# A two-block transformer layer in one kernel: 896 instead of 768 gathered value features, a ring of four blocks, and another order of work where the second block begins

## The chip, the cores and the metric

The kernel runs on one core of a Trainium2 chip. Its time is the device time of one execution in microseconds (us), given as the median of several runs. TensorE (PE in the profile) multiplies matrices and loads their stationary operand (PEld); VectorE (DVE), ScalarE (ACT) and GpSimd (POOL) work on elements; SyncE (SP) issues most DMAs.

## The reference

Two blocks in a row act on 256 tokens of 2048 features. The part that the change touches is the end of the first block, PEER, and the start of the second, in short:

```python
# per token chunk: 8 heads, the 16 best of 16384 experts each
act = jax.nn.gelu(jnp.einsum('chkd,cd->chk', u, zc))     # u = rows of peer_u
v = jnp.take(peer_v, expert, axis=0)
w = (gate * act.astype(jnp.float32)).astype(zc.dtype)
y = jnp.einsum('chk,chkd->cd', w, v)                     # sum of 128 rows of peer_v
...
x = rmsnorm(h + y, norm_f_g)                             # end of the first block
h = rmsnorm_2(x, g_pre_mix)                              # start of the second
proj = jnp.einsum('bsd,de->bse', h, w_in) + b_in
```

## The kernel before

The work is a list of 544 units, walked by every engine in its own program. A unit is one output tile of a matrix product: 1 MB of weights in two halves. SyncE fetches a half into one of eight slots (`raw`); ScalarE rounds it to a high part (`hi`, L997), VectorE subtracts that for a low part (`lo`, L1396), and TensorE multiplies high and low parts with high and low parts of the activations (`ZA`, `ZB`), one pass each. Activations lie feature by feature, 16 tiles of 128 features by 256 tokens (`X` is the residual). An engine's program at step u prepares the weights of units u+2 and u+3 (`prep` in `walk`), evacuates unit u-1, and then does what tables hang on step u.

PEER is computed densely. In the score stage (units 56 to 183) every expert's score is made. In the value stage (units 184 to 311, eight chunks of 16 units) `expert_unit` multiplies scores by `peer_v`, token by token: each unit adds four pieces x to `VM[q]`, for 512 features q, with two halves of 128 tokens (h = 0, 1), and three matmuls each (L670 to L673). The units of a chunk go round q = 0, 1, 2, 3; the last chunk does all of q = 0 first, then 1, 2 and 3, so that q is finished early.

The second token half leaves out its last `WIDE` features: for these GpSimd fetches, for each of 128 picks per token, that token's row of `peer_v` from a copy with rows of `WIDE` features (`v_wide`, made by ScalarE's DMAs in `widen` at the steps of `COPY_AT`) into a ring of `RING` blocks of two rows (`vrow`, `pick`), and VectorE adds them up, weighted, into `vacc` (`picked_dot`, L1727) at the steps of `DOTS_AT`, some units behind the fetches (`picks_by`). `FROM_Q` is the first tile of 128 features that is gathered; for q = 2 the second half has 128 * (FROM_Q - 8) columns left in the matmuls.

At the border, `expert_out(q)` copies the finished sums of q out of PSUM (ScalarE the first token half, L1147, VectorE the second with the gathered sums, L1779 and L1783). `expert_turn(q)` on TensorE (L730, eight transposes) turns them to feature order, after units 300, 304 and 309 and, for q = 3, inside the first group of the second block; `expert_add` adds them to `X` (L1789). `expert_sum(i)` on ScalarE then makes, for each of 16 feature blocks, a square of `X` for the first norm (L1153), `X` times `gf` (L1154), the high operand of the second block from it (L1158), and a square for the second norm (L1161); VectorE makes the low operand (`expert_low`, L1793), GpSimd adds the squares up (`expert_squares`, L2141). The second block starts at unit 312 (`F0`): units 312 and 313 go as a group, k by k, with `expert_turn(3)` after four k. After unit 314 TensorE sums the added squares over the partitions (L755). Semaphores order all of it; an engine that waits holds back everything behind it in its program.

## Time and profile before

| | |
|---|---|
| median of 3 runs | 2969.21 us (2968.11 to 2969.28) |
| profiled execution | 2968.23 us, span 2966.4 us |
| PE / PEld | 2944.9 / 2534.2 us busy |
| DVE / ACT / POOL | 2160.4 / 1565.4 / 976.7 us busy |
| HBM | 268 GB/s over the span |
| granted TensorE clock | 0.999 of full speed (mean) |

Busy is not the same as useful: matmuls overlap, so the time from one start to the next counts, not the duration of one. An idle time is shown with what ended it. In the names, `G<-hi,ZB` is a matmul that writes a bank `G` from `hi` and `ZB`; `M` is the other set of four banks.

### The profile page before, as it was taken

How to read it: one execution, taken by the hardware profiler on the slowest of the kernel's cores; microseconds unless marked ns; L12 is line 12 of the kernel's file. 1: busy time of each engine (PE TensorE's matmuls, PEld its weight loads, DVE VectorE, ACT ScalarE, POOL GpSimd, SP SyncE). 2: the span in 40 equal slices, each digit the busy share in tenths (PEclk: the TensorE clock that was granted, in tenths of full speed). 3: DMA queues.
4: the chain of work that ended last, by engine and by line, in shares of the span. 5: the costliest groups of instructions: out<-in, count | busy, mean ns of one | idle time of the engine just before them, and what ended most of it. 6: DMA issues, size and time to landing. Idle time of an engine off the chain costs nothing.

```text
span 2966.4 us, 42025 instructions
## 1 busy us (share of the span) xinstructions
PE 2944.9 (99%) x15908; PEld 2534.2 (85%) x15908; DVE 2160.4 (73%) x3097; ACT 1565.4 (53%) x2160; POOL 976.7 (33%) x728
## 2 busy tenths in 40 slices
PE   9999999999999999999999999999999999999999
PEld 8888888888888888888887788888888888888888
DVE  8957995555656768888888899897857855545554
ACT  7655464545545545555556656657565544434443
POOL 0013448888883046677664200001512000000000
PEclk9999999999999999999999999999999999999999
DMA  8898979999998889999997555555555565576665
GB/s 298 288 350 299 351 219 266 285 262 259 263 263 253 304 308 372 378 373 377 372 355 258 185 178 171 178 180 190 188 189 177 187 190 191 186 207 193 194 193 149
DMA packets 419834, 747.22 MB, mean 252 GB/s; under 512 B 67248, under 2 KB 243632, under 8 KB 416944
## 3 DMA queue, kind: packets, MB, share of 16 engines
q1 hardware_dynamic: 245792, 593.58, 59.8%
q10 hardware_dynamic: 122640, 100.40, 10.7%
q0 software_dynamic: 51200, 50.56, 7.1%
q8 instruction: 126, 2.06, 0.3%
q14 instruction: 76, 0.62, 0.1%
HBM read 707.57 MB, written 87.17 MB: 268 GB/s over the span
## 4 chain that ended last, share of the span: by engine, by line
PE 88%; DVE 6%; issue 2%; DMA 2%; ACT 1%; POOL 1%; SPq 0%; ACTq 0%; POOLq 0%; DVEq 0%
PE G L608 39%; PE G L612 20%; PE G L673 3%; PE G L670 3%; PE G L672 3%; PE M L670 3%; PE M L672 3%; PE M L673 3%; DVE lo L1396 2%; PE G L699 2%; PE M L699 2%; PE G L698 2%; PE M L698 2%; PE M L700 2%; PE G L700 2%
## 5 line engine op out<-in xcount | busy, mean ns | idle before, releaser
L608 PE MATMUL G<-ZA,hi 128*128 128x512 f32 x5098 | 1765.9, 395 | 9.2 <-DVE lo L1396 4.8
L1396 DVE TENSOR_TENSOR lo<-raw,hi 128x1024 fp32r<-128x1024 f32 x1088 | 1335.4, 1243 | 479.2 <-ACT hi L997 476.3
L997 ACT ACTIVATE hi<-raw 128x1024 fp32r<-128x1024 f32 x1088 | 1128.6, 1055 | 586.2 <-DMA raw<-in_pv 259.1
L612 PE MATMUL G<-ZA,lo 128*128 128x256 f32 x5114 | 1386.5, 278 | 1.0 <-DVE lo L1396 1.0
L608 PEld LDWEIGHTS G<-ZA,hi 128*128 128x128 f32 x5098 | 942.2, 188 | 214.7 <-DVE lo L1396 5.6
L612 PEld LDWEIGHTS G<-ZA,lo 128*128 128x128 f32 x5114 | 961.7, 188 | 20.0 <-DVE lo L1396 1.3
L2104 POOL DMA_INDIRECT g_scratch<-sel,IDX x256 | 433.9, 1695 | 115.6 <-issue 81.7
L1004 ACT ACTIVATE tA<-G 128x256 f32<-128x256 f32 x367 | 139.3, 380 | 509.1 <-PE G L612 497.6
L1402 DVE TENSOR_TENSOR tS<-G,tA 128x256 f32<-128x256 f32 x336 | 141.0, 420 | 255.0 <-ACT tA L1004 251.5
L2120 POOL DMA_INDIRECT vrow<-v_wide,IXV x128 | 172.3, 1346 | 222.1 <-PE G L612 136.8
L2128 POOL DMA_INDIRECT asp<-h_scratch,IXA x128 | 181.3, 1416 | 91.3 <-PE G L670 36.1
L672 PE MATMUL G<-hi,ZB 128*128 128x512 f32 (+1 forms) x512 | 181.3, 363 | 0.0
L673 PE MATMUL G<-hi,ZB 128*128 128x512 f32 (+1 forms) x512 | 179.6, 363 | 0.0
L608 PE MATMUL G<-ZB,hi 128*128 128x512 f32 x512 | 177.4, 394 | 0.7 <-DVE ZB L1476 0.7
L672 PE MATMUL M<-hi,ZB 128*128 128x512 f32 x384 | 150.5, 392 | 0.8 <-ACT hi L997 0.6
L673 PE MATMUL M<-hi,ZB 128*128 128x512 f32 x384 | 149.9, 390 | 0.0
L612 PE MATMUL G<-ZB,lo 128*128 128x256 f32 x512 | 140.9, 277 | 0.0
L1727 DVE SCALAR_TENSOR_TENSOR vacc<-vrow,asp,vacc 128x768 f32<-128x768 f32 x126 | 123.3, 1020 | 2.2
L1812 DVE SCALAR_TENSOR_TENSOR CV<-UC,col,CV 128x256 f32<-128x256 f32 x240 | 117.1, 488 | 6.6
L608 PEld LDWEIGHTS G<-ZB,hi 128*128 128x128 f32 x512 | 95.6, 188 | 22.8 <-DVE ZB L1476 1.0
L670 PE MATMUL G<-lo,ZB 128*128 128x512 f32 (+1 forms) x512 | 112.8, 362 | 0.0
L673 PEld LDWEIGHTS G<-hi,ZB 128*128 128x128 f32 x512 | 96.4, 188 | 16.8
(368 smaller groups left out, 2750.9 us busy)
## 6 DMA issues: line engine op xcount, KB each, us to landing
raw<-in_pu SPq DMA_DIRECT2D x256, 512.0 KB, 4.9
raw<-in_pv SPq DMA_DIRECT2D x256, 512.0 KB, 7.5
raw<-in_w_in SPq DMA_DIRECT2D x192, 512.0 KB, 3.5
raw<-in_w_up SPq DMA_DIRECT2D x128, 512.0 KB, 3.5
raw<-in_w_down SPq DMA_DIRECT2D x128, 512.0 KB, 5.1
v_wide<-in_pv ACTq DMA_DIRECT2D x96, 512.0 KB, 6.8
raw<-in_w_out SPq DMA_DIRECT2D x32, 512.0 KB, 5.7
raw<-in_wq SPq DMA_DIRECT2D x32, 512.0 KB, 5.5
```

The lines of the kernel that those rows point to most:

```text
L608: pe.matmul(G[:, 0:512], w, Z[:, k, :], start=first, stop=False, skip_group_check=True)
L612: m = pe.matmul(G[:, 0:256], lo[raw_slot(POS[u][p])][:, k % 8, :], weights(u, p)[1][:, k, 0:256], start=False, stop=last, skip_group_check ...
L670: m = pe.matmul(G[:, 0:e], zhi, vlo, start=False, stop=c == 7 and n == 3 and x == 3, skip_group_check=True)
L672: pe.matmul(G[:, 0:e], zhi, vhi, start=c == 0 and n == 0 and x == 0, stop=False, skip_group_check=True)
L673: pe.matmul(G[:, 0:e], zlo, vhi, start=False, stop=False, skip_group_check=True)
L997: act.activation(hi[w][:, :, :], raw[r].rearrange("p (k n) -> p k n", k=8), ACT.Copy).then_inc(s_hi, 1)
L1004: act.activation(tA[b % 3][:, :], GB[b % 4][:, 256:512], ACT.Copy).then_inc(s_low, 1)
L1396: dve.tensor_tensor(lo[r][:, :, :], raw[r].rearrange("p (k n) -> p k n", k=8), hi[w][:, :, :].bitcast(F32), ALU.subtract).then_inc(s_lo, 1)
L1402: dve.tensor_tensor(dst, GB[b % 4][:, 0:256], tA[b % 3][:, :], ALU.add).then_inc(s_join, 1)
L2104: pool.indirect_dma_start(scr, bass.IndirectOffsetOnAxis(IDX[:, t, k:k + 1], 0), sel[:, t, k:k + 1], None, compute_op=ALU.add).then_inc(s_ ...
L2120: pool.indirect_dma_start(vrow[:, slot_of(b), k, :], None, vwide, bass.IndirectOffsetOnAxis(IXV[:, at:at + 1], 0)).then_inc(s_pick[b % 2], 16)
L2128: pool.indirect_dma_start(asp[:, at:at + 1], None, hflat, bass.IndirectOffsetOnAxis(IXA[:, at:at + 1], 0)).then_inc(s_pick[b % 2], 16)
```

## The change

`WIDE` becomes 896, so `FROM_Q` is 9 and the second half of q = 2 has 128 columns; `v_wide` gets 16 more column copies, placed at every second step from 67 to 97. The ring has four blocks, and the sums stand three units behind. `expert_out` for q = 0 and 1 is done by ScalarE alone, and for q = 3 on ScalarE at the start of step 312. The operands of the second block are made straight from the residual with the product of the two gains (`gfpm`), before the squares, at the steps of `HIGH_AT`; the square, the scaling of `X` and the second square follow at the steps of `SQUARE_AT`, those of the blocks 8 to 15 at step 312.

```diff
--- before.py
+++ after.py
@@ -167,15 +167,15 @@
 TAIL_END = [7, 13, 18, 22]
 
 V_LAST = VB[KEPT - 1]
-WIDE = 768
+WIDE = 896
 FROM_Q = 16 - WIDE // 128
 BLOCK = 2
 PIECES = 128 // BLOCK
-RING = 5
+RING = 4
 PICK_BASE = 2048
 
 COPY_AT = {}
-for _n, _u in enumerate(sorted(list(range(4, 40)) + list(range(8, 38, 2)) + list(range(66, 156, 2)))):
+for _n, _u in enumerate(sorted(list(range(4, 40)) + list(range(8, 38, 2)) + list(range(66, 156, 2)) + list(range(67, 99, 2)))):
     COPY_AT.setdefault(_u, []).append(_n)
 PITCH = 33 * 1024
 COPIES = sum(len(n) for n in COPY_AT.values())
@@ -214,7 +214,7 @@
 
 DOTS_AT = {}
 for _b in range(PIECES):
-    _u = min(v for v in range(VB[0], F0) if picks_by(v) >= 2 * BLOCK * (_b + 1)) + 4
+    _u = min(v for v in range(VB[0], F0) if picks_by(v) >= 2 * BLOCK * (_b + 1)) + 3
     DOTS_AT.setdefault(_u, []).extend(range(BLOCK * _b, BLOCK * _b + BLOCK))
 
 
@@ -225,7 +225,10 @@
 
 D_LAST = DNB[3]
 TURN_AT = (V_LAST + 4, V_LAST + 8, V_LAST + 13)
-SUMS_AT = {V_LAST + 4 * q + 5 + n: t for q in range(3) for n, t in enumerate(((4 * q, 4 * q + 1), (4 * q + 2,), (4 * q + 3,)))}
+HIGH_AT = {V_LAST + 4 * q + 5 + n: t for q in range(2) for n, t in enumerate(((4 * q, 4 * q + 1), (4 * q + 2,), (4 * q + 3,)))}
+HIGH_AT.update({V_LAST + 14: (8, 9), V_LAST + 15: (10, 11), F0: range(12, 16)})
+SQUARE_AT = {V_LAST + 4 * q + 6 + n: t for q in range(2) for n, t in enumerate(((4 * q, 4 * q + 1), (4 * q + 2,), (4 * q + 3,)))}
+SQUARE_AT[F0] = range(8, 16)
 
 
 def up_split_at(u):
@@ -344,7 +347,7 @@
         col = sb("col", [128, NCOL])
         sp4 = sb("sp4", [128, 3, 8])
         rtok = sp4[:, 0, 0:2]
-        gpp, warm = sb("gpp", [128, 16]), sb("warm", [128, 1])
+        gpp, gfpm, warm = sb("gpp", [128, 16]), sb("gfpm", [128, 16]), sb("warm", [128, 1])
         io16 = sb("io16", [128, 256], BF16)
         r1 = region(1024, "r1_mem", [("R1", [128, T], F32)], [("IXV", [128, 128], U32), ("IXA", [128, 128], U32)])
         r3 = region(1024, "r3_mem", [("R3", [128, T], F32)], [("gsp", [128, 128], F32), ("asp", [128, 128], F32)])
@@ -665,7 +668,7 @@
                             if not e:
                                 continue
                             zhi, zlo = (ZB[:, 4 * n + x, at:at + 128] for at in (128 * h, 256 + 128 * h))
-                            vhi, vlo = whi[:, 0:e // 256, :, x, :], wlo[:, 0:e // 256, :, x, :]
+                            vhi, vlo = (w[:, 0:e // 256, :, x, :] if e > 128 else w[:, 0, 0, x, :] for w in (whi, wlo))
                             if low:
                                 m = pe.matmul(G[:, 0:e], zhi, vlo, start=False, stop=c == 7 and n == 3 and x == 3, skip_group_check=True)
                             else:
@@ -722,8 +725,9 @@
 
             def expert_turn(q):
 
-                pe.wait_ge(s_vea, q + 1)
-                pe.wait_ge(s_ved, q + 1)
+                pe.wait_ge(s_vea, (2, 4, 5, 6)[q])
+                if q >= 2:
+                    pe.wait_ge(s_ved, q - 1)
                 for i in range(4 * q, 4 * q + 4):
                     for h in range(2):
                         at = 128 * (i % 4)
@@ -1144,18 +1148,23 @@
             def expert_out(q):
                 act.wait_ge(s_mm, done(V_LAST + 4 * q + 3))
                 act.wait_ge(s_za, 64)
-                act.activation(by_token(q, 0), VM[q][0][:, :], ACT.Copy).then_inc(s_vea, 1)
-
-            def expert_sum(i):
+                for h in range(2 if q < 2 else 1):
+                    act.activation(by_token(q, h), VM[q][h][:, :], ACT.Copy).then_inc(s_vea, 1)
+
+            def expert_high(i):
                 act.wait_ge(s_vad, i // 2 + 1)
+                act.wait_ge(s_gpp, 3)
+                r = min(RING - 1, (512 * i + 511) // (BLOCK * WIDE))
+                act.wait_ge(s_dot, 128 - BLOCK * (RING - 1 - r))
+                act.activation(ZA[:, i, 0:256], X[:, i, :], ACT.Copy, scale=gfpm[:, i:i + 1]).then_inc(s_zih, 1)
+
+            def expert_square(i):
                 if i >= 2:
                     act.wait_ge(s_acc, 2 * i + 12)
                 act.activation((tQ[0] if i else acc[0])[:, :], X[:, i, :], ACT.Square).then_inc(s_sqr, 1)
+                act.wait_ge(s_zi, i + 1)
                 act.activation(X[:, i, :], X[:, i, :], ACT.Copy, scale=C("gf", i)).then_inc(s_xg, 1)
                 act.wait_ge(s_xg, i + 1)
-                r = min(RING - 1, (512 * i + 511) // (BLOCK * WIDE))
-                act.wait_ge(s_dot, 128 - BLOCK * (RING - 1 - r))
-                act.activation(ZA[:, i, 0:256], X[:, i, :], ACT.Copy, scale=C("gpm", i)).then_inc(s_zih, 1)
                 if i >= 2:
                     act.wait_ge(s_acc, 2 * i + 13)
                 act.activation((tQ[1] if i else acc[1])[:, :], X[:, i, :], ACT.Square).then_inc(s_sqr, 1)
@@ -1249,7 +1258,8 @@
                 if u in range(V_LAST + 4, F0, 4):
                     expert_out((u - V_LAST) // 4 - 1)
                 if u == F0:
-                    act.wait_ge(s_ved, 4)
+                    expert_out(3)
+                    act.wait_ge(s_ved, 2)
                 walk(u, evac, prep)
                 for c, n in SPLIT_AT.get(u, ()):
                     gate_split(c, (2 * n, 2 * n + 1))
@@ -1266,10 +1276,10 @@
                     act.wait_ge(s_mm, done(u - 1))
                     down_squares((u - D_LAST) // 4 - 1, 0)
                     down_squares((u - D_LAST) // 4 - 1, 1)
-                if u == V_LAST + 14:
-                    expert_out(3)
-                for i in SUMS_AT.get(u, range(12, 16) if u == F0 else ()):
-                    expert_sum(i)
+                for i in HIGH_AT.get(u, ()):
+                    expert_high(i)
+                for i in SQUARE_AT.get(u, ()):
+                    expert_square(i)
                 if u == F0:
                     act.wait_ge(s_mm, done(F0 - 1))
                     act.dma_start(neg[:, :], ins["con"][:, CEND + 384:CEND + 768]).then_inc(s_mn, 16)
@@ -1790,7 +1800,7 @@
 
             def expert_low(i):
                 dve.wait_ge(s_zih, i + 1)
-                dve.scalar_tensor_tensor(out=ZA[:, i, 256:512], in0=X[:, i, :], scalar=C("gpm", i),
+                dve.scalar_tensor_tensor(out=ZA[:, i, 256:512], in0=X[:, i, :], scalar=gfpm[:, i:i + 1],
                                          in1=ZA[:, i, 0:256].bitcast(F32), op0=ALU.mult, op1=ALU.subtract).then_inc(s_zi, 1)
 
             def gate_split(c, pairs):
@@ -1854,8 +1864,8 @@
             for u in range(N + 1):
                 if u == SG + 19:
                     depthwise(taps, 1000)
-                if u in range(V_LAST + 4, F0, 4):
-                    expert_out((u - V_LAST) // 4 - 1)
+                if u == V_LAST + 12:
+                    expert_out(2)
                 if u == F0:
                     expert_add(6)
                     expert_add(7)
@@ -1874,11 +1884,11 @@
                     down_base()
                 if u == V_LAST + 13:
                     expert_out(3)
-                if u in range(V_LAST + 5, F0, 4):
+                if u in (V_LAST + 5, V_LAST + 9, V_LAST + 14):
                     q = (u - V_LAST - 5) // 4
                     expert_add(2 * q)
                     expert_add(2 * q + 1)
-                for i in SUMS_AT.get(u, range(12, 16) if u == F0 else ()):
+                for i in HIGH_AT.get(u, ()):
                     expert_low(i)
                 if u in (0, 1):
                     squares_sum(u)
@@ -1886,6 +1896,8 @@
                     dve.wait_ge(s_con, 32)
                     dve.tensor_tensor(gpp[:, :], col[:, COL0["gpost"]:COL0["gpost"] + 16],
                                       col[:, COL0["gpmlp"]:COL0["gpmlp"] + 16], ALU.mult).then_inc(s_gpp, 1)
+                    dve.tensor_tensor(gfpm[:, :], col[:, COL0["gf"]:COL0["gf"] + 16],
+                                      col[:, COL0["gpm"]:COL0["gpm"] + 16], ALU.mult).then_inc(s_gpp, 1)
                 if u == 61:
                     decode()
                 if u == 3:
@@ -2142,7 +2154,7 @@
 
             for u in range(N + 1):
                 walk(u, evac, lambda h: None)
-                for i in SUMS_AT.get(u, range(12, 16) if u == F0 else ()):
+                for i in SQUARE_AT.get(u, ()):
                     if i:
                         expert_squares(i)
                 if u == F0:
```

On TensorE, a value unit of q = 2 and the start of its second product group before; L672 and L673 are the high and low scores with the high weights, `G` the banks of q = 2:

```order
L672 MATMUL G<-hi,ZB 128x512
L673 MATMUL G<-hi,ZB 128x512
L672 MATMUL G<-hi,ZB 128x256
L673 MATMUL G<-hi,ZB 128x256
L672 MATMUL G<-hi,ZB 128x512
L673 MATMUL G<-hi,ZB 128x512
L672 MATMUL G<-hi,ZB 128x256
L673 MATMUL G<-hi,ZB 128x256
```

The same place after the change:

```order
L675 MATMUL G<-hi,ZB 128x512
L676 MATMUL G<-hi,ZB 128x512
L675 MATMUL G<-hi,ZB 128x128
L676 MATMUL G<-hi,ZB 128x128
L675 MATMUL G<-hi,ZB 128x512
L676 MATMUL G<-hi,ZB 128x512
L675 MATMUL G<-hi,ZB 128x128
L676 MATMUL G<-hi,ZB 128x128
```

Every second pair is half as wide; nothing else moves on TensorE.

On ScalarE, the steps 303 and 304 before, from the conversions of step 303 to those of step 304; `A<-G` is the copy of the finished sums of q = 1 (first token half), the four passes ahead of it are those of feature block 3:

```order
L997 ACTIVATE hi<-raw 128x1024 x2
L1153 ACTIVATE tQ<-X 128x256
L1154 ACTIVATE X<-X,col 128x256
L1158 ACTIVATE ZA<-X,col 128x256
L1161 ACTIVATE tQ<-X 128x256
L1147 ACTIVATE A<-G 128x512
L997 ACTIVATE hi<-raw 128x1024 x4
```

and after, where block 3 has its operand and block 2 its squares there:

```order
L1001 ACTIVATE hi<-raw 128x1024 x2
L1159 ACTIVATE ZA<-X,gfpm 128x256
L1164 ACTIVATE tQ<-X 128x256
L1166 ACTIVATE X<-X,col 128x256
L1170 ACTIVATE tQ<-X 128x256
L1152 ACTIVATE A<-G 128x512 x2
L1001 ACTIVATE hi<-raw 128x1024 x2
```

The copies of q = 1 are two instead of one, and the passes between conversions and copies are as many as before.

On ScalarE, from the copy of the sums of q = 2 on (step 308) before; `A<-M` is the copy of q = 3, the groups of four are feature blocks 8 and following:

```order
L1147 ACTIVATE A<-G 128x512
L997 ACTIVATE hi<-raw 128x1024 x4
L1153 ACTIVATE tQ<-X 128x256
L1154 ACTIVATE X<-X,col 128x256
L1158 ACTIVATE ZA<-X,col 128x256
L1161 ACTIVATE tQ<-X 128x256
L1153 ACTIVATE tQ<-X 128x256
L1154 ACTIVATE X<-X,col 128x256
L1158 ACTIVATE ZA<-X,col 128x256
L1161 ACTIVATE tQ<-X 128x256
L997 ACTIVATE hi<-raw 128x1024 x2
L1147 ACTIVATE A<-M 128x512
```

and after, from the same copy on, up to the operands of blocks 12 to 15 at step 312:

```order
L1152 ACTIVATE A<-G 128x512
L1001 ACTIVATE hi<-raw 128x1024 x2
L1164 ACTIVATE tQ<-X 128x256
L1166 ACTIVATE X<-X,col 128x256
L1170 ACTIVATE tQ<-X 128x256
L1001 ACTIVATE hi<-raw 128x1024 x4
L1159 ACTIVATE ZA<-X,gfpm 128x256 x2
L1001 ACTIVATE hi<-raw 128x1024 x2
L1159 ACTIVATE ZA<-X,gfpm 128x256 x2
L1152 ACTIVATE A<-M 128x512
L1001 ACTIVATE hi<-raw 128x1024 x2
L1159 ACTIVATE ZA<-X,gfpm 128x256 x4
```

Before, the two conversions of step 310 stood behind the eight passes for blocks 8 and 9; now they stand ahead of the first pass for block 8 (the last two of the four); the copy of q = 3 stands behind the operands of blocks 8 to 11 and two more conversions; the passes for the squares of blocks 8 to 15, 24 of them, come behind the last row.

## Rows read from the trace of the kernel before

Durations and starts are in us from the span's start, unless a column is a mean in ns.

**Rows 1.** The page, busy us by engine, share of the span, instructions
```profile
PE 2944.9 (99%) x15908; PEld 2534.2 (85%) x15908; DVE 2160.4 (73%) x3097; ACT 1565.4 (53%) x2160; POOL 976.7 (33%) x728
```

**Rows 2.** Stretches: us, busy (x) of PE, PEld, DVE, ACT, POOL, clock, DMA, GB/s
```profile
1060.00:1585.00 525.00, 523.07 (x2456) 435.91 (x2455) 448.94 (x489) 272.45 (x288) 346.94 (x252) 1.00 1.00 363
...
1602.00:1638.00 36.00, 32.10 (x165) 26.92 (x164) 32.25 (x37) 23.82 (x41) 11.89 (x14) 0.95 0.69 229
1638.00:1664.00 26.00, 20.27 (x112) 16.61 (x111) 18.85 (x22) 23.00 (x42) 14.34 (x20) 1.00 0.52 176
```

**Rows 3.** Timeline of PE, value units: start us, us, engine, line, op
```profile
1115.26 0.39 PE L672 MATMUL G<-hi,ZB 128*128 128x512 f32 x1
...
1120.70 0.39 PE L672 MATMUL G<-hi,ZB 128*128 128x512 f32 x1
...
1121.15 0.28 PE L672 MATMUL G<-hi,ZB 128*128 128x256 f32 x1
...
1121.39 0.40 PE L672 MATMUL G<-hi,ZB 128*128 128x512 f32 x1
...
1124.87 0.40 PE L672 MATMUL M<-hi,ZB 128*128 128x512 f32 x1
```

**Rows 4.** Groups by shape, PE: xcount, busy us, mean ns, idle before
```profile
L673 PE MATMUL G<-hi,ZB 128*128 128x256 f32 x128 | 35.6, 278 | 0.0
```

**Rows 5.** Timeline of PEld: loads of four one-column matmuls, and the next
```profile
2374.00 0.53 PEld L939 LDWEIGHTS M<-con,R 128*128 128x128 f32 x4
2374.46 0.19 PEld L608 LDWEIGHTS G<-ZA,hi 128*128 128x128 f32 x1
```

**Rows 6.** Timeline of PE: f32 products of 128 columns
```profile
2959.46 3.74 PE L883 MATMUL G<-R,U 128*128 128x128 f32 x32
```

**Rows 7.** The page, groups of DVE at 768 and at 256 columns
```profile
L1727 DVE SCALAR_TENSOR_TENSOR vacc<-vrow,asp,vacc 128x768 f32<-128x768 f32 x126 | 123.3, 1020 | 2.2
L1812 DVE SCALAR_TENSOR_TENSOR CV<-UC,col,CV 128x256 f32<-128x256 f32 x240 | 117.1, 488 | 6.6
```

**Rows 8.** Waits in the value stage: us in total, times, longest us
```profile
PE M L670 <- DVE lo L1396: 1.0, 1, 1.0
...
ACT hi L997 <- DMA raw<-in_pv: 249.7, 195, 4.8
```

**Rows 9.** The page, DMA issues of weights, median us to landing
```profile
raw<-in_pu SPq DMA_DIRECT2D x256, 512.0 KB, 4.9
raw<-in_pv SPq DMA_DIRECT2D x256, 512.0 KB, 7.5
raw<-in_w_in SPq DMA_DIRECT2D x192, 512.0 KB, 3.5
```

**Rows 10.** Timeline and waits of PE at the border
```profile
1608.69 1.06 PE L730 MATMUL G<-con,A 128*128 128x128 f32 x8 [1.61 <-DVE A L1779]
...
1628.04 1.21 PE L670 MATMUL M<-lo,ZB 128*128 128x512 f32 x4 [1.21 <-DVE lo L1396]
1630.33 1.94 PE L730 MATMUL G<-con,A 128*128 128x128 f32 x8 [1.07 <-DVE A L1783]
...
1641.44 0.50 PE L608 MATMUL G<-ZA,hi 128*128 128x512 f32 x1 [2.86 <-DVE lo L1396]
...
PE G L608 <- DVE ZA L1793: 2.9, 3, 1.6
```

**Rows 11.** Timeline of ACT, DVE and POOL at the border
```profile
1635.95 0.42 ACT L1153 ACTIVATE tQ<-X 128x256 f32<-128x256 f32 x1 [3.80 <-DVE X L1789]
...
1639.08 1.99 ACT L997 ACTIVATE hi<-raw 128x1024 fp32r<-128x1024 f32 x2
...
1635.25 1.27 DVE L1789 TENSOR_TENSOR X<-X,G 128x512 f32<-128x512 f32 x2
...
1637.70 2.28 POOL L2141 TENSOR_TENSOR acc<-acc,tQ 128x256 f32<-128x256 f32 x3 [0.51 <-ACT tQ L1161]
...
1648.85 5.51 POOL L2141 TENSOR_TENSOR acc<-acc,tQ 128x256 f32<-128x256 f32 x5 [0.92 <-ACT tQ L1153]
```

## The prediction

> **What bounds the kernel now.** I read the busy shares first, then a table of stretches, then the waits and the timeline of single units. The busy shares say that the matmuls fill 2944.9 us of a span of 2966.4 [rows 1]. So nothing that another engine saves counts unless TensorE waits for it, and the first question is how much TensorE work the change takes away. The stretches say where TensorE does wait: in the long value stage (1060 to 1585 us) it is idle 1.9 us of 525, while the DMA share is 1.00 at 363 GB/s and VectorE is busy 449; in the two stretches around the border to the second block it is idle 36.0 - 32.1 = 3.9 and 26.0 - 20.3 = 5.7 us, and in the first of them the granted clock falls to a mean of 0.95 [rows 2]. The profiled execution took 2968.2 us against a median of 2969.2 for the runs, so I work against 2968.2 and add 1 at the end.
>
> **The narrow matmuls.** In 32 of the 128 value units the second token half has 256 columns left, in 12 matmuls each: 384 matmuls, recorded as three groups of 128 [rows 4]. They become 128 wide. A full unit of 24 matmuls of 512 columns takes 1120.70 - 1115.26 = 5.44 us, 0.227 a matmul. The next, with 12 narrow ones, takes 4.17; less 12 x 0.227 that leaves 0.121 for a narrow one, and two of them start 0.24 apart for both [rows 3]. No matmul of 128 columns in this operand kind is in the trace, so its slot is bounded. Low end: by slope, (0.227 - 0.121)/256 columns, a 128 wide one takes 0.121 - 0.053 = 0.068. High end: the f32 products of 128 columns, which come as two records each, 32 records in 3.74 us, that is 0.112 a record and 0.224 a product [rows 6]. The nearest row is about the weights: every matmul here has its own load, and four matmuls of one column, which stream next to nothing, still have their loads spread over 0.46 us until the next load begins, 0.115 each [rows 5]. A load can hide under the matmul before it, but not two loads under one short matmul, and behind a narrow matmul there is always another load. So I take 0.113 for the slot (0.112 to 0.115 are the two rows): 384 x (0.121 - 0.113) = 3 us saved, of the 20 that the columns alone suggest. The ends are 384 x 0.053 = 20 saved and 384 x (0.224 - 0.121) = 40 lost.
>
> **The gathered side.** 128 rows of 896 instead of 768 columns are fetched and added up. One VectorE sum takes 1.020 us at 768 columns and its sister at 256 takes 0.488 [rows 7]: 1.04 ns a column, so 0.133 more each, 128 x 0.133 = 17 us of VectorE. It had 525 - 449 = 76 us free in the stage, so the mean load goes from 86 to 89%. The fetches bring 128 x 128 x 512 bytes = 8.4 MB more on 363 GB/s x 525 us = 191 MB, 4.4%. TensorE waited for a late low part once in this stage, for 1.0 us; ScalarE stood 250 us for weights to land [rows 8], 7.5 us after issue at the median [rows 9], so conversion already runs right behind the landing. The sums move one unit nearer to their fetches and the ring loses a block. A block is four fetches, so 1.85 units; ring slots now come free 3 blocks + the fetch later, 5.5 units after a block is complete, instead of 7.4, and the sums stand 3 instead of 4 units behind. The margin shrinks by a unit of some 4.4 us; what is queued behind a late slot on GpSimd is only the next fetches, which nobody needs for three units. I put 2 us on the stage for later landings and later conversions (0 to 8: eight such units with the full 1.0 us wait of rows 8). The 16 additional copies of 512 KB run in the score stage, whose units last 16 x (0.227 + 0.121) = 5.6 us and whose weights land in 4.9 [rows 9], against a value stage that lives with 7.5; they are hidden there, at nothing (0 to 2, what the whole value stage loses at its higher load). The new 16-column product on VectorE near the start lies beside a unit of 5.6 us: nothing.
>
> **The border.** What goes [rows 10]:
> 1.6 us before the second turn, where TensorE waited for a VectorE copy that ScalarE now makes ahead of its squares;
> 1.2 us for a low part of the weights, late because the last two sums stood in front of it on VectorE, now one unit earlier;
> 1.1 us before the third turn, same reason;
> the half clock behind these two idles: 0.05 of 36 us is 1.8 us, taken as 1.7;
> 2.9 us for the low weights of the first group, whose ScalarE conversion started at 1639.08 because it stood behind four passes per feature block, the first of which had waited 3.8 us for the residual [rows 11]; these conversions now come before that wait;
> 2.9 us in three waits for the last operands, which now need one ScalarE pass after the residual instead of three.
> Together 11.4 us.
>
> What is late next. First, the fourth turn. It needs a ScalarE copy that now stands behind the work of two units. Counted from the end of the third turn (zero): the last weights of that step are issued when the unit ahead of the turn ends, at -0.9, land 3.5 later [rows 9], and are converted by 2.6 + 1.0 + 1.2, with 0.5 for issue and hand-over 5.3; the residual sums behind them on VectorE take 1.3 [rows 11], 6.6; two operands on ScalarE at 0.42 by such a pass [rows 11] and a hand-over, 7.5; two conversions in 2.0 [rows 11], 9.5; two operands, 10.4; the copy, twice as wide, 11.0. TensorE has two units of 12 x 0.227 = 2.7 and four steps of the group, 2 x (0.227 + 0.121) = 0.7 each, and stands there at 8.2. A turn itself is eight transposes and about 0.9 us [rows 10]. So it waits 2.8 us. Second, the totals of the squares. Both squares of eight feature blocks now come after the last operand. From the end of the fourth turn: residual sums 1.3, four operands 1.8, first square 0.4, then 16 additions on GpSimd at 2.28/3 = 0.76 [rows 11], 12.2, in all 15.7; ScalarE's 24 passes of some 0.4, 9.6, fit beside the additions. TensorE reaches the totals after 12 steps and a unit, 8.4 + 5.6 = 14.0. It waits some 2 us with the hand-over. For other small waits I take 0.5. New waits: 5.3. The border nets 11.4 - 5.3 = 6.1 us. The ends are a gain of 11.4, if neither new wait appears, and a loss of 1.0, if the additions take 5.51/5 = 1.10 each as five of them did before [rows 11], 5.4 us more, and the half clock comes back with its 1.7.
>
> Rows 11 have additions of 0.76 and of 1.10 us. The Trainium skill (GPSIMD Engine Reference, 1. Specifications) says that GpSimd shares its SBUF interfaces with VectorE and is in contention with VectorE instructions that have two SBUF inputs. The subtractions of the weight conversion are of that kind; by that rule the additions run at 0.76 while ScalarE is in its 24 passes, since VectorE then gets nothing to subtract, and the result stays 2962; at 1.10 it would be 2967.
>
> **Sum.** -3.0 + 2.0 - 6.1 = -7.1, so 2961.1 for the profiled execution and 2962 for the median. Its own range is 2956 to 2970.
>
> **Rivals.**
> *The narrow matmul follows its columns* (slot 0.068). For it: the slope between 512 and 256 columns is clean. Against it: rows 5. It saves 20 us; TensorE then asks for weights 4% faster from a DMA at share 1.00, so I put 5 us of supply waits: -20 + 5 - 6 = -21, 2948.
> The Trainium skill (TensorE: Matmul & The Clock Gate, section Back-to-back issue gap) gives about 81 ns per matmul for a stream of load and matmul pairs at 128 columns; by it the saving is an estimated 15 us and the time 2951. The same sentence gives 131 ns at 512 columns, where this trace has 227, so the measurement decides against the sentence here.
> *The narrow matmul loses the single pass* (slot 0.224): this operand kind runs once through the array at 512 and 256 columns, and nothing shows that it does so at 128; if it takes as long as an f32 product of that width, each of the 384 costs 0.103 more. That is +40, the supply waits go (0), the border gains its 6: +34, 3003. For it: the kernel's trace has no such matmul below 256 columns. Against it: f32 products differ already in their number of records. It decides from a slot of 0.121 + 4/384 = 0.131 on; above that the border's gain is spent. This is the rival on the other side.
> *The DMA becomes the bound of the value stage*: 8.4 MB at 363 GB/s would be 23 us. For it: share 1.00. Against it: the queue of weights is limited by free slots, and TensorE waited twice in 525 us. +23 - 3 - 6 = +14, 2983.
>
> **Chances.** Forecast 0.55, columns 0.13, single pass lost 0.25, DMA bound 0.07. A measurement of this kernel tells 0.2%, 5.9 us, from no change. Faster by more: 0.13 and 0.32 of the forecast's 0.55, 0.45. Within: 0.20 of the forecast. Slower: 0.25 + 0.07 + 0.03 = 0.35. The range 2955 to 3005 holds the forecast, the DMA case and most of the lost pass, 0.8; it leaves out the columns.
>
> **What would show it.** A value unit with narrow matmuls of 4.08 us (forecast), 3.5 (columns) or 5.4 (pass lost) in the timeline, seen at once. At the border: no wait of the second turn, of the third, of the first group's low weights or of the last operands; a wait of TensorE for a ScalarE copy at the fourth turn, and one for GpSimd's additions before the totals; clock 1.00 throughout. In the value stage: sums of 1.15 us, GB/s near 375, waits of TensorE below 5 us in total. The prediction is wrong if the narrow slot is not near 0.113, or if the value stage waits grow past 8 us.

## The result, and the profile after

The changed kernel takes 2975.28 us (median of 12 runs, 2973.20 to 2980.58) against 2969.24 us (12 runs of the kernel before on the same chip): the ratio is 1.0024, 95% interval 1.0017 to 1.0032. It is slower, by 6 us in the medians and 5 to 9 by the interval, where I had forecast 7 us faster. The profiled execution has a span of 2973.4 us, 7.0 more than before.

I cut both spans at the same matmuls, whose starts are in the timeline of TensorE: the first of the value stage, the first of its unit 112 (of 128), the first of unit 304 of the program, the first total of squares, and the first total of the norm behind the short attention.

| stretch, us | before | changed | difference |
|---|---|---|---|
| start to the value stage | 1056.5 | 1055.7 | -0.8 |
| value units 0 to 111 | 501.8 | 511.1 | +9.3 |
| units to 304 | 44.4 | 44.4 | 0.0 |
| unit 304 to the totals (the border) | 60.0 | 55.6 | -4.4 |
| totals to the next norm | 343.2 | 346.7 | +3.5 |
| the rest | 960.4 | 959.8 | -0.6 |

Two things happened that I had not priced: the value stage lost much more than 2 us, and most of the border's gain was returned behind the totals.

The page of the changed kernel, busy us by engine (before: [rows 1]):

```profile
PE 2948.6 (99%) x15908; PEld 2535.4 (85%) x15908; DVE 2175.6 (73%) x3096; ACT 1570.7 (53%) x2162; POOL 965.6 (32%) x728
```

The stretches of [rows 2] again, in the changed kernel (us, busy of PE, PEld, DVE, ACT, POOL, clock, DMA share, GB/s):

```profile
1060.00:1585.00 525.00, 516.93 (x2415) 427.42 (x2414) 455.99 (x483) 268.07 (x284) 320.65 (x248) 1.00 1.02 374
1602.00:1638.00 36.00, 34.13 (x183) 28.99 (x182) 32.89 (x35) 27.88 (x50) 16.56 (x15) 1.00 0.75 239
1638.00:1664.00 26.00, 22.49 (x109) 19.03 (x108) 18.79 (x22) 19.35 (x39) 12.12 (x15) 0.87 0.52 173
```

In the value stage TensorE is idle 8.1 us instead of 1.9, though its matmuls are cheaper. The DMA share, which stood at 1.00, is 1.02, and its rate went from 363 to 374 GB/s: 3% more rate for 4.4% more bytes. The clock of the third stretch is 0.87, because the granted clock stood at half, 1.2 instead of 2.4 GHz, for 6.8 us from 1648.2 us on, during TensorE's wait for the fourth turn. It stood at half once more, for 3.4 us from 1201.1 us on, just behind a wait of 1.9 us in the value stage; at half speed these 3.4 us cost 1.7.

The unit with narrow matmuls, timeline of TensorE (before: [rows 3]):

```profile
1120.03 0.39 PE L675 MATMUL G<-hi,ZB 128*128 128x512 f32 x1
...
1120.49 0.22 PE L675 MATMUL G<-hi,ZB 128*128 128x128 f32 x1
1120.54 0.28 PE L676 MATMUL G<-hi,ZB 128*128 128x128 f32 x1
1120.66 0.45 PE L675 MATMUL G<-hi,ZB 128*128 128x512 f32 x1
1120.94 0.39 PE L676 MATMUL G<-hi,ZB 128*128 128x512 f32 x1
...
1124.10 0.44 PE L675 MATMUL M<-hi,ZB 128*128 128x512 f32 x1
```

It lasts 4.07 us (forecast 4.08). A group of four products, two wide and two narrow, repeats after 0.69 us (0.70 before). The second narrow one begins 0.055 behind the first and the wide one 0.115 behind that, but the next wide one comes 0.285 later instead of 0.23: what the narrow ones save is nearly all given back there.

The last of these long steps falls into the next unit, twelve wide matmuls on `M`. That unit's first and the first matmul behind it, in the changed kernel and then before:

```profile
1124.10 0.44 PE L675 MATMUL M<-hi,ZB 128*128 128x512 f32 x1
...
1126.90 0.39 PE L675 MATMUL M<-hi,ZB 128*128 128x512 f32 x1
```

```profile
1107.09 0.40 PE L672 MATMUL M<-hi,ZB 128*128 128x512 f32 x1
...
1109.82 0.39 PE L672 MATMUL M<-hi,ZB 128*128 128x512 f32 x1
```

It takes 2.80 us instead of 2.73, in every kernel here that has the narrow matmuls and in none that hasn't. In three decimals the shortest pair of units takes 4.064 + 2.802 us instead of 4.163 + 2.730: 0.027 less, not 0.10. So the 32 narrow units save 0.9 us, and the 28 of them among the units 0 to 111 save 0.8.

The waits of TensorE and ScalarE in the value stage (us in total, times, longest; before: [rows 8]), and the page's group of VectorE's sums (before: [rows 7]):

```profile
ACT hi L1001 <- DMA raw<-in_pv: 242.9, 184, 5.5
...
PE M L673 <- DVE lo L1406: 5.4, 7, 1.9
...
PE M L675 <- ACT hi L1001: 1.8, 3, 0.9
PE G L675 <- ACT hi L1001: 0.9, 2, 0.5
```

```profile
L1737 DVE SCALAR_TENSOR_TENSOR vacc<-vrow,asp,vacc 128x896 f32<-128x896 f32 x126 | 139.9, 1152 | 2.2
```

TensorE's waits total 8.1 us, past the 8 us that the prediction gave as the sign of its failure. The releaser named is VectorE's low half. Read alone, that row says that VectorE is to blame, whose sums are 0.13 us longer. The experiments below say otherwise.

At the border, the waits of TensorE from 1590 to 2000 us in the changed kernel:

```profile
PE M L734 <- ACT A L1152: 3.1, 1, 3.1
PE G L734 <- DVE A L1793: 1.9, 1, 1.9
PE G L615 <- DVE lo L1406: 1.5, 2, 1.3
PE M L851 <- ACT O L1238: 0.7, 1, 0.7
PE G L611 <- DVE lo L1406: 0.4, 1, 0.4
```

The wait at the fourth turn is there (3.1, forecast 2.8). The third turn still waits for VectorE (1.9), which I had struck out. The third row, for `lo`, and the fourth, for `O`, stand behind the totals, in a stretch that I had not looked at. The waits of the second turn, of the late low part and of the first group's low weights are gone, but for 0.4 us of the first group's, and so are those for the last operands.

### The profile page after: what moved, and what is told of

Its sections match the earlier page's. It is cut to its first block, busy times and chain, and to the rows that moved or that the text cites. A ratio compares the mean times of both kernels' runs of the same rounds, so it can differ in the third digit from the quotient of the medians.

```text
span 2973.4 us, 42041 instructions
## 1 busy us (share of the span) xinstructions
PE 2948.6 (99%) x15908; PEld 2535.4 (85%) x15908; DVE 2175.6 (73%) x3096; ACT 1570.7 (53%) x2162; POOL 965.6 (32%) x728
## 4 chain that ended last, share of the span: by engine, by line
PE 89%; DMA 4%; DVE 3%; issue 2%; ACT 1%; POOL 1%; SPq 0%; ACTq 0%; POOLq 0%; DVEq 0%
PE G L611 42%; PE G L615 21%; DMA raw<-in_pv 3%; PE M L673 2%; PE G L673 2%; PE G L676 2%; PE G L675 2%; PE M L675 2%; PE M L676 2%; PE G L702 2%; PE M L702 2%; PE M L703 2%; PE G L703 2%; PE M L701 2%; PE G L701 2%
## 5 line engine op out<-in xcount | busy, mean ns | idle before, releaser
L615 PE MATMUL G<-ZA,lo 128*128 128x256 f32 x5114 | 1389.0, 278 | 1.5 <-DVE lo L1406 1.5
L615 PEld LDWEIGHTS G<-ZA,lo 128*128 128x128 f32 x5114 | 962.9, 188 | 21.0 <-DVE lo L1406 2.1
L2116 POOL DMA_INDIRECT g_scratch<-sel,IDX x256 | 443.0, 1731 | 113.5 <-issue 80.3
L2132 POOL DMA_INDIRECT vrow<-v_wide,IXV x128 | 165.8, 1295 | 247.4 <-PE G L615 129.3
L2140 POOL DMA_INDIRECT asp<-h_scratch,IXA x128 | 165.2, 1291 | 93.4 <-PE G L673 33.5
L675 PE MATMUL G<-hi,ZB 128*128 128x512 f32 (+1 forms) x512 | 178.9, 359 | 0.9 <-ACT hi L1001 0.9
L676 PE MATMUL G<-hi,ZB 128*128 128x512 f32 (+1 forms) x512 | 171.7, 362 | 0.0
L1737 DVE SCALAR_TENSOR_TENSOR vacc<-vrow,asp,vacc 128x896 f32<-128x896 f32 x126 | 139.9, 1152 | 2.2
L615 PE MATMUL G<-ZB,lo 128*128 128x256 f32 x512 | 140.9, 277 | 0.0
L673 PE MATMUL G<-lo,ZB 128*128 128x512 f32 (+1 forms) x512 | 112.6, 362 | 0.0
```

The lines of the kernel that those rows point to most:

```text
L615: m = pe.matmul(G[:, 0:256], lo[raw_slot(POS[u][p])][:, k % 8, :], weights(u, p)[1][:, k, 0:256], start=False, stop=last, skip_group_check ...
L673: m = pe.matmul(G[:, 0:e], zhi, vlo, start=False, stop=c == 7 and n == 3 and x == 3, skip_group_check=True)
L675: pe.matmul(G[:, 0:e], zhi, vhi, start=c == 0 and n == 0 and x == 0, stop=False, skip_group_check=True)
L676: pe.matmul(G[:, 0:e], zlo, vhi, start=False, stop=False, skip_group_check=True)
L1737: dve.scalar_tensor_tensor(out=to, in0=row_, scalar=w, in1=to, op0=ALU.mult, op1=ALU.add).then_inc(s_dot, 1)
L2116: pool.indirect_dma_start(scr, bass.IndirectOffsetOnAxis(IDX[:, t, k:k + 1], 0), sel[:, t, k:k + 1], None, compute_op=ALU.add).then_inc(s_ ...
```

## The experiments

Times of the kernel before shift by a microsecond or two from chip to chip, so each run's ratio is to the runs of before that it shared. The kernels built on the border alone have 768 gathered features, a ring of five blocks and sums four units behind, as before.

**1. One part of the change at a time.** Four kernels: the changed one with the border alone, the one before with the gathered side alone, the one before with the ring alone, and the changed one with its 384 narrow matmuls left 256 wide.

```diff
 border alone (from the changed kernel)      gathered side alone (from the one before)
-WIDE = 896                                  +WIDE = 896
+WIDE = 768                                  +RING = 4, sums 3 units behind, 112 copies
+RING = 5, sums 4 units behind, 96 copies    +narrow operand for e == 128
```

> The changed kernel with the value stage of the kernel before (768 features, ring of five, sums four units behind, 96 copies, 256-column matmuls), so the new border alone. Theory S (the value stage lost 12 us to late supply, the border kept only 1 to 2 us of its gain because later units wait): between the 200th score unit and the last value chunk it takes what the kernel before takes, 502 us, and the whole is 1.5 to 6 us faster than before, 2963 to 2968. Rival B (the border itself is what made the change slower, the value stage only shifted the waits): 2970 or more.

Measured: 2967.52, ratio 1.0001 [0.9992, 1.0010]; value units 0 to 111 take 500.6 us. The stage is as theory S has it, but the gain of 1.5 to 6 us is not there: the time falls into the expected range only because the kernel before took 2966.9 in the same series.

> The kernel before with the value stage of the change alone (896 features, ring of four, sums three behind, 112 copies, 128-column matmuls), the border as before. Theory S: the value stage takes 511 instead of 502 us and the whole 2975 to 2981. Rival B: within 3 us of the kernel before.

Measured: 2978.85 (5 runs), ratio 1.0044 [1.0031, 1.0057]; value units 0 to 111 take 510.2 us.

```diff
 ring alone (from the one before)            wide matmuls kept (from the changed kernel)
-RING = 5                                    -e = min(512, max(0, 128 * (FROM_Q - 4 * q))) if h else 512
+RING = 4, sums 3 units behind               +e = min(512, max(0, 128 * (FROM_Q + 1 - 4 * q))) if h else 512
```

> The kernel before with a ring of four blocks and sums three units behind, nothing wider. Within theory S, if the ring's timing is what makes conversions late (GpSimd waited 30 us for sums in the changed kernel, 0.4 before): value stage 506 us or more, whole 2973 or more. If the bytes and the longer sums do it: value stage within 1.5 us of 502, whole within 2 us of before.

Measured: 2967.43, ratio 1.0004 [0.9995, 1.0012]; value units 0 to 111 take 500.1 us. With the narrower rows the ring and the earlier sums cost nothing that can be measured, although GpSimd now waits 6.9 us for sums there. No run has the wider rows with a ring of five, so what the ring adds to them is not shown.

> The changed kernel, but the 384 narrow matmuls stay 256 columns wide (128 of them computed for nothing; the output uses the gathered ones). If the narrow slot is bound by the weight load, a unit goes from 4.07 back to 4.17 us and the whole is the same as the changed kernel within 3 us, since part of the 3 us of TensorE time is waiting anyway. If narrow matmuls cost more than they seem (a slower restart after each), it is faster than the changed kernel by over 3 us.

Measured: 2974.52, ratio 1.0031 [1.0019, 1.0043], value units 512.8 us: 1.7 us more than in the changed kernel, 0.8 of it by the narrow matmuls' own spacing, and far from the 20 us that the columns alone would be worth. The rest is waits, which differ by as much between profiles of like kernels (below).

So the gathered side costs 13 us by itself (9 to 17 by the interval), and the border gives nothing by itself, though its profile reaches the totals 4.3 us sooner than before (55.7 us instead of 60.0 from unit 304). The two do not add up to the 7 us of the whole change. In the profile of the gathered side alone the old border takes 62.7 us instead of 60.0: TensorE waits 5.8 us for the first group's low weights, not 2.9, and within that wait the granted clock falls to half, for 6.8 us. The new border takes 55.6 beside the wider rows. So with the wider rows the new border is worth more than alone; the two ratios' intervals touch, and no further run tests it.

**2. Bytes or VectorE?** The wider rows bring both. In the first kernel all 896 columns are fetched and only 768 summed; in the second 768 are fetched (from 96 copies, not 112) and 896 summed. The first leaves 128 columns out of its output, the second has wrong values in them.

```diff
 short sum:   -vrow[:, slot_of(b), k % BLOCK, :]      +vrow[:, slot_of(b), k % BLOCK, 0:768]
 short fetch: -vrow of [128, RING, BLOCK, WIDE]       +vrow of [128, RING, BLOCK, 768], v_wide of 768 columns
```

> The changed kernel, with 896 columns of every row fetched and copied as in it, but only 768 of them weighted and added on VectorE (from the third sum on; 128 columns are left out of the output). The value stage took 511.1 us in the changed kernel and 501.8 before, though its narrow matmuls give 2.8 back, so some 12 us of its supply are lost. Theory V (VectorE's wider sums, 128 x 0.13 = 17 us more in the stage, delay the low halves of the value weights): the sums go back to about 1.02 us, the value stage to 499 to 502 us, and the time to about 2964 us. Theory D (the wider rows take DMA bandwidth from the value weights): the stage stays at 509 to 511 and the time at 2973 to 2976. If both share it, about 2969.

Measured: 2972.96, ratio 1.0023 [1.0014, 1.0032].

> The changed kernel, with 768 columns of every row fetched (and 96 copies instead of 112), while VectorE's sums stay 896 columns wide (each reads 128 columns of its block's other row, so the last columns of the output are not the reference's). It is the mirror of the run with short sums. Theory V: value stage 509 to 511 us, time 2973 to 2976. Theory D: the landing of a half of a value weight, which rose from 7.52 to 8.32 us (issue to the start of its high half) with the wider rows, returns to 7.5, the stage to 499 to 502 us and the time to about 2964.

Measured: 2966.05, ratio 0.9999 [0.9990, 1.0008]. Both come out with theory D, the second not wholly: 503.6 us in the value units where 499 to 502 were expected.

The software queue of the fetches from 1060 to 1585 us (packets, MB, share of the 16 engines), in before, the short sum and the short fetch:

```profile
q0 software_dynamic: 14092, 49.63, 25.0%
```

```profile
q0 software_dynamic: 13952, 57.33, 28.2%
```

```profile
q0 software_dynamic: 14053, 49.53, 24.9%
```

The 500 us from 1060 to 1560 us in before, the changed kernel, the short sum and the short fetch, one row each (columns as above):

```profile
1060.00:1560.00 500.00, 498.07 (x2346) 415.20 (x2345) 426.99 (x465) 260.33 (x275) 331.69 (x241) 1.00 1.01 366
```

```profile
1060.00:1560.00 500.00, 491.93 (x2299) 406.55 (x2298) 431.13 (x456) 254.38 (x270) 305.10 (x236) 1.00 1.02 375
```

```profile
1060.00:1560.00 500.00, 491.31 (x2303) 406.16 (x2302) 418.84 (x457) 255.57 (x270) 313.84 (x237) 1.00 1.02 375
```

```profile
1060.00:1560.00 500.00, 495.65 (x2338) 412.48 (x2337) 440.21 (x466) 259.56 (x274) 319.72 (x240) 1.00 1.01 365
```

The matmuls begun in the same 500 us are 2346, 2299, 2303 and 2338. Taking VectorE's extra work away wins back 4 of the 47 lost; taking the bytes away wins back 39. In us from the timelines (value units 0 to 111): 511.1 changed, 510.3 with short sums, 503.6 with short fetches, 500.6 with the border alone. The last has no narrow matmuls, which save 0.8; so the bytes alone cost 510.3 + 0.8 - 500.6 = 10.5 us, VectorE's columns alone 3.8, and both 11.3, of which 1.7 are the half clock at 1201 us.

How far can one profile be trusted? Nine kernels here fetch and sum 768 columns, with no narrow matmul, and differ in nothing else that touches these units but the ring; their units 0 to 111 take 499.2 to 501.8 us in eight, and 504.0 in one (the short chain below). The four that fetch 896 take 510.2 to 512.8. So the cost of the bytes is clear, to some 3 us, and that of VectorE's columns is not: 503.6 lies among the nine. The device times say the same: the ratio is 1.0023 with the bytes and 0.9999 without, 7 us apart, with intervals that don't meet.

With the short sums TensorE still waited 5.1 us for VectorE's low half and 2.7 for ScalarE's high half, with VectorE's load below its old level (419 us of 500 instead of 427): the low half was late because its weights were. From the issue of a half of a value weight to the start of its high half it takes 7.82 us on average in before, 8.51 in the changed kernel, 8.75 with short sums and 7.84 with short fetches; the four kernels with the wider fetch have 8.49 to 8.75, all others 7.74 to 7.93. These means are over all 256 halves; the 7.52 and 8.32 in the expectation above are lower by 0.2 to 0.3, with the same rise.

Is a DMA share of 1.00 the sign to look for, then? Two stretches of the score stage in the changed kernel, while `v_wide` is copied, say no:

```profile
448.00:492.00 44.00, 44.00 (x256) 38.47 (x255) 25.57 (x33) 21.80 (x32) 37.29 (x23) 1.00 1.10 338
536.00:580.00 44.00, 44.00 (x255) 38.51 (x254) 25.57 (x33) 22.19 (x32) 38.20 (x20) 1.00 1.13 356
```

The 16 more copies raise the share there from 0.99 and 1.06 to 1.10 and 1.13, and TensorE does not wait at all. What differs is the slack: from 448 to 888 us of before, ScalarE waited 58 us in 440 for weights to land, in 58 of some 160 conversions; in the value stage it was 250 us in 540, in 195 of some 250 [rows 8].

**3. Where the border's gain goes.** Behind the first total of squares a chain runs to the first scaled unit: root on ScalarE, reciprocal, product, second root, second reciprocal, scaling; behind it stand ScalarE's next high half and VectorE's next low half, for which TensorE waits. A table load of 1.28 us stands just ahead of the root on ScalarE. First the timelines of before and of the border alone, at the total on TensorE, the root on ScalarE and the low half on VectorE:

```profile
1662.77 1.03 PE L755 MATMUL M<-acc,con 128*128 128x256 f32 x4
...
1663.41 0.48 ACT L1344 ACTIVATE R<-M,col 128x256 f32<-128x256 f32 x1 [0.29 <-PE M L755]
...
1673.37 1.23 DVE L1396 TENSOR_TENSOR lo<-raw,hi 128x1024 fp32r<-128x1024 f32 x1 [2.87 <-ACT hi L997]
```

```profile
1657.38 1.13 PE L759 MATMUL M<-acc,con 128*128 128x256 f32 x4 [1.14 <-POOL acc L2153]
1673.58 0.39 PE L615 MATMUL G<-ZA,lo 128*128 128x256 f32 x1 [0.76 <-DVE lo L1406]
...
1662.32 0.47 ACT L1354 ACTIVATE R<-M,col 128x256 f32<-128x256 f32 x1
...
1672.30 1.23 DVE L1406 TENSOR_TENSOR lo<-raw,hi 128x1024 fp32r<-128x1024 f32 x1 [2.87 <-ACT hi L1001]
```

The total comes 5.4 us sooner, the root and the low half only 1.1 us: ScalarE, which ends its squares at 1656.5, makes four high halves and loads the table first. Before, the low half was ready 11.8 us behind the total and TensorE took it at 15.1, so it did not wait. Now it is ready at 16.1, and TensorE waits. The slack that hid the chain was 3.3 us, and the sooner total used it up.

That is not the whole of the +4.3 us. Matmul by matmul from the first total on, the border alone falls 2.8 us behind at this low half and the next, within 24 us; 0.6 more creep in over the next 40 us, with no wait recorded; and 0.9 come at two waits for ScalarE in the short attention, for `zs` at 114 us (L869) and for `O` at 122 us (L851, 0.68 us instead of 0.29). In the changed kernel the three parts are 2.0, 0.6 and 0.9. No run was made to find the cause of the last two. The remedy to test for the first is the chain's order.

```diff
 the root first (ScalarE; on VectorE the first reciprocal likewise)
+if u == F0 + 2: wait for the total, R3 = Sqrt(...)
 walk(u, evac, prep)
-if u == F0 + 2: wait for the total, R3 = Sqrt(...)
```

> The border of the changed kernel alone, on 768 gathered features (2967.5 us), with one thing moved: the square root and the reciprocal that begin the norm behind the border stand ahead of the two splits of weights of their step, on ScalarE and on VectorE, not behind them. In that kernel TensorE reached the totals 5.4 us earlier than before, but the root began only 1.1 us earlier (1662.3 against 1663.4), and 2.8 to 3.5 us of the gain were lost again behind the totals, in waits of L615 for the low half. Theory N (the norm's chain, from the root to ScalarE's first split behind it, sets that wait, and ScalarE's order holds the root back): the root begins at about 1660.2, the waits of L615 behind the totals fall from 2.0 us to under 0.3, and the time to about 2965. Rival (what is given back has another cause, such as the squares' work itself or VectorE's order, or the later splits make TensorE wait as long as the root is earlier): time unchanged, 2967 to 2968.

Measured: 2965.45, ratio 0.9995 [0.9986, 1.0004]. The root begins at 1659.05, 2.5 us behind the total instead of 4.9, but the two splits now stand inside the chain, and the waits of L615 are still 1.8 us in total. So the chain was lengthened by most of what its start had gained: from the root to the scaling it takes 8.7 us instead of 6.7. The time is as theory N said, its reason is not: the waits were to fall under 0.3.

```diff
 the tight chain (from the root first), VectorE, step F0 + 2
-reciprocal; evacuations; split; split; product; second reciprocal
+reciprocal; evacuations; product; split; second reciprocal; split
```

> The kernel with the root first (768 gathered features), with the rest of the norm's chain on VectorE moved up too: the product behind GpSimd's first step stands ahead of the two splits of that step, and the second reciprocal between them. In that kernel the chain from the root to the scaling of the first unit took 8.7 us (1659.05 to 1667.74), because VectorE's two splits (2.4 us) stood inside it, and TensorE waited 1.8 us for L615's low halves 16 to 23 us behind the totals. Theory N (this chain sets those waits): 7.4 to 7.6 us, the waits fall from 1.8 to about 0.6 us and the time by about 1.2 us, to 2964 to 2965. Rival: the second split is now late for TensorE and the time stays at 2965.5 or rises.

Measured: 2964.61, ratio 0.9995 [0.9986, 1.0003]. From the root to the scaling it takes 8.0 us (8.7 with the root first, 7.4 to 7.6 expected), and one wait of 1.2 us (0.6 expected) is left for the low half:

```profile
1657.90 0.47 ACT L1265 ACTIVATE R<-M,col 128x256 f32<-128x256 f32 x1
...
1665.89 0.43 DVE L1417 TENSOR_TENSOR tS<-tS,R 128x256 f32<-128x256 f32 x1 [0.62 <-POOL R L2200]
```

```profile
PE G L615 <- DVE lo L1407: 1.2, 1, 1.2
```

The three kernels of this series have ratios of 1.0001, 0.9995 and 0.9995, with waits of 2.0, 1.8 and 1.2 us at L615. The waits shrink as the theory says; the times do not tell the three apart.

**4. Taking the new waits away.** The rest of the border's waits are at the third and fourth turn and before the totals.

```diff
 the lean border (from the root first)
+ScalarE takes the last product at the start of step 311
+second square with the scale inside; the scaling of blocks 8 to 15 on VectorE
+squares of blocks 8 to 11 ahead of the copies of 12 to 15
```

> The kernel with the root first, and three edits more: ScalarE takes the last turn's product at the start of step 311 (not behind its two splits and two copies: the fourth turn waited 1.6 us for it); the squares of the scaled block are made with the scale inside the instruction, and the scaling of blocks 8 to 15 goes to VectorE, which was idle for 8.6 us there; the squares of blocks 8 to 11 begin before the copies of 12 to 15, so that GpSimd's sixteen additions of 0.775 us (12.4 us without a break from 1644.9 on, which the totals waited for by 1.1 us) start at about 1641. Theory N: no wait at the fourth turn (1.6), none before the totals (1.1), less than 0.5 us behind them (2.8 to 3.5 before): 5 to 6 us under the border alone, 2961 to 2963 us. Rival: what is gained in front of the totals is given back behind them as in that kernel, and the time stays within 1.5 us of 2965 to 2967.

Measured: 2967.60, ratio 1.0006 [0.9997, 1.0015]. The fourth turn comes 10.8 us behind the third, without its wait. But GpSimd's additions now run beside VectorE's low halves, and TensorE waits 4.6 us for block 12. The wait in its table of waits, and the low halves of blocks 10 and 11 on VectorE, first in this kernel beside the additions, then in the border alone, where GpSimd was idle:

```profile
PE G L611 <- DVE ZA L1808: 4.6, 1, 4.6
```

```profile
1638.54 1.85 DVE L1808 SCALAR_TENSOR_TENSOR ZA<-X,gfpm,ZA 128x256 fp32r<-128x256 f32 x2
```

```profile
1641.13 0.87 DVE L1803 SCALAR_TENSOR_TENSOR ZA<-X,gfpm,ZA 128x256 fp32r<-128x256 f32 x2
```

The two take 1.85 us instead of 0.87. Within that wait the granted clock falls to half, for 6.8 us, and from unit 304 to the totals it takes 59.1 us (55.7 in the border alone). The two low halves hold up the residual sums of blocks 12 to 15 behind them, and with the squares of 10 and 11 ahead of the copies on ScalarE the operands of block 12 come too late.

```diff
 split sums (from the root first): the last product early; low halves of 12 and 13 ahead of
 the splits; VectorE adds the scaled squares of blocks 11 to 15
```

> The kernel with the root first (768 gathered features), with three edits: ScalarE takes the last turn's product at the start of step 311; VectorE makes the low halves of blocks 12 and 13 ahead of its two splits of step 312; of the sixteen additions of squares behind the last copies, VectorE takes five (the scaled squares of blocks 11 to 15, with the scale inside ScalarE's square), so that GpSimd has 11 x 0.775 = 8.5 us of them instead of 12.4. No square stands ahead of the copies of 12 to 15, since in the lean border GpSimd's additions beside VectorE's low halves doubled these (0.92 us each instead of 0.44) and TensorE waited 4.6 us for block 12. Theory N: no wait at the fourth turn (3.1 in the profile of the root first, 13.1 us between the last two turns against 10.8 in the lean border), none before the totals, the totals some 2.5 us earlier; behind them 1 to 2 us of waits remain: 2962.5 to 2964. Rival G (behind the totals everything gained ahead of them is lost again, whatever is done): 2965 to 2966.

Measured: 2967.00, ratio 0.9998 [0.9989, 1.0007]. The fourth turn no longer waits, but TensorE waits 1.5 us for the low half of a late block and 1.6 for VectorE's additions before the totals, and 2.1 at L615, not less than with the root first (1.8).

```diff
 early third turn (from the split sums): the third product's 256 token columns are copied by
 ScalarE, and VectorE adds its gathered part one step earlier
```

> The split sums, and the third turn fed earlier: ScalarE copies the 256 columns that VectorE copied, right behind its own copy, and VectorE's sum of the gathered part stands one step earlier, so that the product is whole when TensorE comes to the third turn (2.1 to 2.6 us of wait in the border alone, the root first and the lean border). Theory N: that wait goes and the time falls by 1.5 to 2.5 us under the split sums, to 2961 to 2963. Rival G: the wait returns at the fourth turn or behind the totals, and the time is within 0.7 us of the split sums.

Measured: 2966.02, ratio 1.0000 [0.9991, 1.0009]. The wait at the third turn fell from 2.1 to 1.4 only: in front of VectorE's sum at 1624.65 us stand two of the picked sums (2.87 us) and two splits (2.89), not its copy.

```diff
 short chain (from the early third turn): tight chain; low halves of 12 to 15 ahead of the
 splits; the scaling of blocks 8 to 15 on VectorE
```

> The kernel with the split sums and the early third turn, with the same short chain, with all four low halves of blocks 12 to 15 ahead of VectorE's splits of step 312 (TensorE waited 1.7 us for block 14 in it), and with the scaling of blocks 8 to 15 on VectorE instead of ScalarE (8 x 0.40 us, so that ScalarE, which ended its squares at 1655.0, is free some 3 us earlier and the root does not begin 2.85 us behind the first total but about 1.6). Theory N: no wait of TensorE between the fourth turn and the totals, less than 1 us behind them; about 3 us under the kernel that it is made from, 2962 to 2963.5. Rival G (what is gained ahead of the totals comes back as a wait elsewhere): 2965 to 2966.

Measured: 2966.86, ratio 0.9995 [0.9986, 1.0004]. Behind the totals no wait for a low half is left, as the chain theory has it, and the creep is gone with it. But VectorE and GpSimd now share the squares, and TensorE waits for them in front of the totals:

```profile
PE M L759 <- DVE acc L1921: 4.2, 1, 4.2
```

Within this wait the granted clock falls to half, for 6.8 us from 1658.8 on, and that costs 2.4 us behind the totals: the stretch to the next norm still takes 346.2 us (343.2 before). This profile is also the one with 504.0 us in the value units.

No kernel here is faster than the one before by more than the measurement tells. The tight chain has the lowest median, 2964.6 against 2967.4 of before in the same series, and its interval still holds 1. The intervals of the six kernels built on the border alone all lie below that of the changed kernel (from 1.0017 on).

## Why the prediction was wrong

*The narrow matmul, 0.113 a slot.* The unit was right, 4.07 us against 4.08, and the choice among the rivals too: not the columns, and the single pass was not lost. The gain was not: the next unit gives 0.07 us back, so a narrow matmul saves 0.002 us and not 0.008, and the term of 3 us is worth 0.9.

*"I put 2 us on the stage for later landings and later conversions."* This is the step that failed. It measured 10.5 us for the bytes (11.3 with VectorE's columns and a half clock of 1.7). I had the rows that say so, the DMA share of 1.00 [rows 2] and ScalarE waiting for 195 of some 250 landings, 250 us in all [rows 8], and put them aside because TensorE hardly waited and the queue of weights is limited by free slots. Both were true of the stage before, and it stood just short of the edge all the same. The DMA rival (23 us, chance 0.07) had the right mechanism; its price was about twice too high, since the rate still rose. An estimate with the rate of after: 191 + 8.4 MB at 374 GB/s take 532 us instead of 525, 7 us of the 10.5.

*The ring and the sums' distance.* Right that it costs next to nothing, as far as the run with the narrower rows tells; it was my reason for the 2 us, and the ring alone shows none of it.

*The copies and the product near the start, nothing.* Right: the value stage begins at 1055.7 us, and in all profiles here between 1055.1 and 1058.3.

*The border, -6.1.* The mechanism in front of the totals was half right: 4.4 us came (4.3 with the border alone), with the fourth turn's wait as forecast, but with the third turn's wait still there and, in the changed kernel, with a half clock of 6.8 us, so that TensorE did not reach the totals ahead of the additions and had no wait there. What the term left out is behind the totals: +3.5 us in the changed kernel, +4.3 with the border alone, 2.0 and 2.8 of them at the low halves behind the norm's chain. I ended the count at the last wait that I saw, and not at the next point where TensorE meets the other engines. As measured, the border is worth -0.9 and not -6.1. This is the second step that failed.

*The additions on GpSimd at 0.76.* They took 12.80 us for 16, 0.80 each. VectorE did get something to do beside the first of them, the last four low halves. The contention is taken up at the end.

As measured the sum is -0.8 (start) + 10.1 - 0.8 (value units) - 4.4 + 3.5 (border) - 0.6 (rest) = +7.0.

*The ranges.* The ends that I gave to the terms, 8 for the stage and a loss of 1.0 at the border, add up to -3 + 8 + 1 = +6, so 2975; my own range of 2956 to 2970 was cut narrower than its parts. The measured 2975.3 lies in the wide range, 2955 to 3005, by luck: that range reached so far for the lost single pass, and none of the cases stood at 2975.

## What to carry to other kernels

Where the DMA share is 1.00 and the engine that takes the transfers waits for most of them, added bytes cost time even if the matmul engine barely waits: price them at the DMA's rate first, as an upper end, and look for slack second. A share of 1.00 or more alone does not say so, as the score stage shows. Don't believe the engine named in the wait, since a late conversion inherits a late landing. When a matmul gets shorter, time the units behind it too. A gain in front of a meeting point counts only up to the slack of the chain behind it, so follow the other engines' chain to the next place where the matmul engine takes something from it. And when work moves to an idle engine, ask which busy engine it will slow down.

## What the runs showed of the hardware

Two narrow matmuls begin 0.055 us apart, the wide one 0.115 behind, and the next wide one 0.285 behind that, not 0.23: the loads of a narrow pair begin 0.11 us apart, and a group of four takes 0.69 us with the narrow pair 128 columns wide and 0.70 with 256. VectorE and GpSimd slow each other. In the border alone VectorE's low halves of 256 columns (two operands in SBUF) are recorded at 0.48 us with GpSimd idle and 0.96 beside its additions, and these at 0.73 with VectorE idle and 0.92 beside them, and the two then proceed in step, one of each every 0.88 us:

```profile
1645.39 3.60 DVE L1803 SCALAR_TENSOR_TENSOR ZA<-X,gfpm,ZA 128x256 fp32r<-128x256 f32 x4
...
1644.93 12.40 POOL L2153 TENSOR_TENSOR acc<-acc,tQ 128x256 f32<-128x256 f32 x16 [14.82 <-ACT tQ L1164]
```

The Trainium skill (SBUF — State Buffer, SBUF: two separate sides) calls the port pair that the two share an exclusive lock, held for a whole instruction by whichever starts first, where VectorE's instruction has two inputs in SBUF or runs in a mode with two ports. The doubling of VectorE's time agrees in kind; but one of each without contention takes 0.40 + 0.70 = 1.10 us from start to start, and together they need 0.88, so here they do overlap in part. In the lean border VectorE's multiplication by a column, with a single operand in SBUF, slows as well, and no run tells in which mode it runs: eight beside the additions take 6.03 us, at 0.82 each, against 0.41 for one without:

```profile
1648.01 6.03 DVE L1904 TENSOR_SCALAR X<-X,col 128x256 f32<-128x256 f32 x8
...
1674.50 0.41 DVE L1824 TENSOR_SCALAR CV<-UC,col 128x256 f32<-128x256 f32 x1
```
